# Two transformer blocks on one core: row projections that finish a token half at a time, banks and orders at the seams laid out anew, and two of three products joined into one of 512 columns

## The reference

```python
def first_block(x, mem, ...):
    h = rmsnorm(x, norm_mix)
    fq, fk, fv, ff, gq, gk, gv, gb, ga, gz, sq, sk, sv, gates = split(h @ w_in)
    ya = fox_attention(rmsnorm(fq), rmsnorm(fk), fv, log_sigmoid(ff + bias))   # 4 heads of 128
    yb = rmsnorm(gated_delta_rule(silu(conv(gq, gk, gv)), ...)) * silu(gz)
    yc = stick_breaking_attention(sq, sk, sv)
    g = sigmoid(gates + gate_bias)                                             # 3 x 1024
    x = x + (g[0] * (ya @ w_oa) + g[1] * (yb @ w_ob) + g[2] * (yc @ w_oc)) @ w_out
    x = x + memory_cross_attention(rmsnorm(x), rmsnorm(mem), ...)              # w_mq, w_mkv, w_mo
    return x + conv_ffn(rmsnorm(x), w_up, ffn_conv, w_down)                    # d_ff 2816

def second_block(x, mem, ...):
    x = x + 0.5 * rmsnorm(swiglu(rmsnorm(x), ffn1_w_gate, ffn1_w_up, ffn1_w_down))
    q, k, v, p = split(rmsnorm(x) @ w_in_2)                                    # 512 each
    y = concat(moba_attention(q, k, v), multiscale_pool(p)) @ w_out_2          # 8 heads of 64
    x = x + rmsnorm(y)
    x = x + rmsnorm(memory_cross_attention_2(rmsnorm(x), rmsnorm(mem), ...))   # 4 heads of 256
    return x + 0.5 * rmsnorm(swiglu(rmsnorm(x), ffn2_w_gate, ffn2_w_up, ffn2_w_down))
```

## Time and profile before

| what | value |
|---|---|
| median of three runs | 1312.2 us |
| profiled execution, its own time | 1314.68 us |
| its span on the core | 1313.0 us |
| mean granted TensorE clock | 0.961 of full speed |
| PE busy | 1220.3 us in 8179 matmuls |
| DVE busy | 721.6 us in 797 instructions |
| ACT busy | 631.4 us in 785 instructions |
| HBM read | 191.82 MB, 147 GB/s over the span |

### The profile page before, as it was taken

The page is one execution under the profiler, slowest core; times in us unless marked ns, Lnnn a source line. Parts: engine busy times, 40 slices in busy tenths (PEclk is TensorE's granted clock), DMA queues, the critical chain, the costliest instruction groups (busy, mean ns, idle before and its releaser), DMA issues. The chain is left out here.

```text
span 1313.0 us, 19388 instructions
## 1 busy us (share of the span) xinstructions
PE 1220.3 (93%) x8179; PEld 1116.4 (85%) x8179; DVE 721.6 (55%) x797; ACT 631.4 (48%) x785; POOL 52.5 (4%) x81
## 2 busy tenths in 40 slices
PE   6979999999889989999999999998879987999997
PEld 6967979899888779999889999887857865999985
DVE  6755443643577546788545554445574634555443
ACT  6554434543646746555535444435443634544441
POOL 6001100200000000000000000001000000000000
PEclk9988998999999999999999999998988998999998
DMA  8632222332446434555664555555313424455550
GB/s 241 188 107 97 84 78 73 94 124 97 151 156 209 139 104 157 185 174 189 208 194 157 180 186 172 205 192 167 129 65 114 160 64 144 139 183 193 193 192 32
DMA packets 144142, 194.12 MB, mean 148 GB/s; under 512 B 6136, under 2 KB 121208, under 8 KB 144056
## 3 DMA queue, kind: packets, MB, share of 16 engines
q1 hardware_dynamic: 142856, 188.43, 44.1%
q0 software_dynamic: 1200, 4.46, 1.0%
HBM read 191.82 MB, written 1.05 MB: 147 GB/s over the span
## 5 line engine op out<-in xcount | busy, mean ns | idle before, releaser
L1469 DVE TENSOR_TENSOR wlo<-raw,whi 128x2048 fp32r<-128x2048 f32 x178 | 408.4, 2296 | 293.8 <-ACT whi L1207 293.5
L922 PE MATMUL banks<-xh,whi 128*128 128x256 f32 x1704 | 497.4, 292 | 5.6 <-DVE xl L1486 4.3
L922 PE MATMUL banks<-xl,whi 128*128 128x256 f32 x1704 | 487.3, 286 | 0.0
L922 PE MATMUL banks<-xh,wlo 128*128 128x256 f32 x1704 | 486.9, 286 | 0.0
L1207 ACT ACTIVATE whi<-raw 128x2048 fp32r<-128x2048 f32 x178 | 339.4, 1909 | 203.5 <-PE banks L948 121.1
L922 PEld LDWEIGHTS banks<-xh,whi 128*128 128x128 f32 x1704 | 332.8, 195 | 13.6 <-DVE xl L1486 5.5
L922 PEld LDWEIGHTS banks<-xl,whi 128*128 128x128 f32 x1704 | 332.7, 195 | 1.9 <-issue 1.7
L922 PEld LDWEIGHTS banks<-xh,wlo 128*128 128x128 f32 x1704 | 332.2, 195 | 0.0
L948 PE MATMUL banks<-whi,hh 128*128 128x512 f32 x264 | 102.7, 389 | 0.0
L948 PE MATMUL banks<-wlo,hh 128*128 128x512 f32 x264 | 102.7, 389 | 0.0
L948 PE MATMUL banks<-whi,hl 128*128 128x512 f32 x264 | 102.7, 389 | 0.0
(11 more groups left out here) (362 smaller groups left out, 1538.0 us busy)
## 6 DMA issues: line engine op xcount, KB each, us to landing
raw<-in_w_in SPq DMA_DIRECT2D x40, 1024.0 KB, 5.3
raw<-in_w_up SPq DMA_DIRECT2D x22, 1024.0 KB, 5.1
raw<-in_ffn_w_gate SPq DMA_DIRECT2D x22, 1024.0 KB, 5.4
raw<-in_ffn_w_up SPq DMA_DIRECT2D x22, 1024.0 KB, 5.3
raw<-in_ffn_w_down SPq DMA_DIRECT2D x22, 1024.0 KB, 4.9
raw<-in_w_down SPq DMA_DIRECT2D x11, 1024.0 KB, 4.8
raw<-in_w_out SPq DMA_DIRECT2D x8, 1024.0 KB, 4.9
raw<-in_xa_wkv SPq DMA_DIRECT2D x8, 1024.0 KB, 5.2
```

What stands on the lines that cost most here:

```text
L922: ins = pe.matmul(o, a[:, k, cols_], v[:, k, :], start=(k == 0 and i == 0), stop=(k == KD - 1 and i == 2))
L1469: dve.tensor_tensor(wlo[c % RING][:, :], raw[c % RING][:, :], whi[c % RING][:, :], ALU.subtract).then_inc(dve_done, 1)
```

## The change

**Joined products.** A new kind W takes the place of A in 84 chunks: `fq`, `fk`, `sq`, `sk` and `gz` of the first block, its 12 gate chunks, `mk`, `mq`, the cross attention's keys and queries of the second block, both of its FFNs' gate and up chunks, and the `qk` and `pin` columns of `w_in_2`. `xh` and `xl` lie side by side in `xhl`, so `whi` is multiplied by both in one matmul of 512 columns (L1004 in the changed kernel), and `wlo` by `xh` in one of 256 (L1006): 32 matmuls where there were 48. The result lies in two banks in place of one, and the two halves of a bank, 256 columns each, must be added: `add`, `ga` and `ua`, each a `tensor_reduce` on DVE (L1817, L1824, L1829) that reads 1024 floats of a partition and writes 512. It takes the place of the `copy` on ACT and of the FFN steps' direct reads. The first block's FFN and the convolution stay as they were.

**Half by half.** The last R chunk of a projection does all its products for t = 0 in `mm(c, 0)` and those for t = 1 in `mm(c, 1)`. Residual, `post` steps and norm steps follow for one half at a time, the first beside `mm(c, 1)`.

**Banks.** Each row projection has banks 0 to 3 or 4 to 7, and the transposes of the norm behind it work in the others.

**Orders.** The lanes of the memory attention and of the last cross attention lane are run between the chunks of `w_mo` and `xa_wo_2`, each chunk of which waits for its own heads alone. `w_in_2` starts with the pool's columns; the window sums are a side chain; `w_out_2` takes its rows in the order 2, 3, 0, 1, so that the pool's rows come first. At the FFN seams `nl` goes ahead of the last `add` and of `lo(c + 2)` (`fill_and_turn`).

The diff, cut to its core:

```diff
+    def two_banks():
+
+        turn[0] += 1
+        return (0, 1) if turn[0] % 2 else (2, 3)
...
+    def wide(name, c0, x, evac, banks=None, **k):
+
+        out.append(dict(kind="W", srcs=[((0, 256), kpn(w[name][:, c0:c0 + 256]))], x=x, banks=banks or two_banks(), evac=evac, **k))
...
-    def rows(name, n, x, evac):
-        for j in range(n):
-            out.append(dict(kind="R", j=j, last=j == n - 1, srcs=[((0, 1024), kpn(w[name][256 * j:256 * j + 256, :]))],
-                            x=x, banks=(4, 5, 6, 7), evac=evac if j == n - 1 else None, name=name))
+                            x=x, banks=banks, evac=evac if half else None, **k))
+
+    def rows(name, n, x, evac, base, order=None):
+        for nth, j in enumerate(order or range(n)):
+            out.append(dict(kind="R", j=j, first=nth == 0, last=nth == n - 1,
+                            srcs=[((0, 1024), kpn(w[name][256 * j:256 * j + 256, :]))],
+                            x=x, banks=tuple(range(base, base + 4)), evac=evac if nth == n - 1 else None, name=name))
...
-    ffn(0, "w_up", "w_up", "w_down", DFF)
-    xa_k(3)
-    ffn(1, "ffn1_w_gate_2", "ffn1_w_up_2", "ffn1_w_down_2", 0)
-    xa_v(0)
+            left = KF // 2 - 1 - i
+            if f == 0:
+                b = 2 * (left % 4)
+                cols(gate, 256 * i, "x", (b,), None, f=f, i=i, part="gate")
+                cols(up, c_up + 256 * i, "x", (b + 1,), "ffn", f=f, i=i, part="up")
+            else:
+                b = 4 * ((left + f - 1) % 2)
+                wide(gate, 256 * i, "x", "gate", (b, b + 1), f=f, i=i, part="gate")
+                wide(up, c_up + 256 * i, "x", "ffn", (b + 2, b + 3), f=f, i=i, part="up")
+        rows(down, KF // 2, "h%d" % f, evac, base)
+
+    ffn(0, "w_up", "w_up", "w_down", DFF, "resid", 4)
+    xa_k(3, (2, 3))
+    ffn(1, "ffn1_w_gate_2", "ffn1_w_up_2", "ffn1_w_down_2", 0, "post", 4)
+    xa_v(0, (2, 3))
     win = "w_in_2"
-
+    turn[0] = 0
+    for i in range(2):
+        wide(win, 1536 + 256 * i, "x", "add", to="pin", i=i)
+    for i in (0, 2):
+        wide(win, 256 * i, "x", "add", to="qk", i=i)
     vals(win, 1024, "x", "vcopy", to="bv")
-    for n, i in enumerate((0, 2, 1, 3)):
-        cols(win, 256 * i, "x", (n % 2,), "copy", to="qk", i=i)
-    for i in range(2):
-        cols(win, 1536 + 256 * i, "x", (i % 2,), "copy", to="pin", i=i)
-    rows("w_out_2", 4, "y5", "post")
-    xa_v(1)
+    for i in (1, 3):
+        wide(win, 256 * i, "x", "add", to="qk", i=i)
+    rows("w_out_2", 4, "y5", "post", 0, (2, 3, 0, 1))
+    xa_v(1, (4, 5))
     for i in range(4):
-        cols("xa_wq_2", 256 * i, "x", (i % 2,), "copy", to="xq", i=i)
-    rows("xa_wo_2", 4, "y5", "post")
-    ffn(2, "ffn2_w_gate_2", "ffn2_w_up_2", "ffn2_w_down_2", 0)
+        wide("xa_wq_2", 256 * i, "x", "add", ((6, 7), (0, 1), (2, 3), (0, 1))[i], to="xq", i=i)
+    rows("xa_wo_2", 4, "y5", "post", 0)
+    ffn(2, "ffn2_w_gate_2", "ffn2_w_up_2", "ffn2_w_down_2", 0, "post", 0)
...
+        if ev == "resid":
+            pl.add("dve", "resid", c, 0)
+            pl.add("act", "ns", norm_after(c), 0)
+        elif ev == "post":
+            post(c, 0)
+        for s in mid:
+            place(s)
...
         elif ev == "resid":
-            for t in range(NT):
-                pl.add("dve", "resid", c, t)
+            pl.add("dve", "resid", c, 1)
+            pl.add("act", "nr", norm_after(c), 0)
+            pl.add("act", "ns", norm_after(c), 1)
+            pl.add("dve", "nd", norm_after(c), 0)
+            pl.add("act", "nr", norm_after(c), 1)
+            pl.add("dve", "nd", norm_after(c), 1)
         elif ev == "post":
-            for t in range(NT):
-                pl.add("act", "post1", c, t)
-                pl.add("dve", "post0", c, 1 - t)
-            pl.add("act", "post_r", c)
-            for t in range(NT):
-                pl.add("dve", "post2", c, t)
+            post(c, 1)
...
+    def post(c, t):
+
+        pl.add("act", "post1", c, t)
+        pl.add("dve", "post0", c, t)
+        pl.add("act", "post_r", c, t)
+        pl.add("dve", "post2", c, t)
+        if t and norm_after(c):
+            norm_scale(norm_after(c))
+
+    def norm_scale(name, *ts):
+        for t in ts or range(NT):
             pl.add("act", "ns", name, t)
-        pl.add("act", "nr", name)
-        for t in range(NT):
+            pl.add("act", "nr", name, t)
             pl.add("dve", "nd", name, t)
 
-    def norm_turn(name, into="x"):
+    def fill_and_turn(c, name, base):
+
+        pl.add("act", "hi", c + LEAD)
+        mm(c, early=False, keep=True)
+        norm_turn(name, base)
+        pl.add("dve", "add", c)
+        pl.add("dve", "lo", c + LEAD)
+
+    def norm_turn(name, base, into="x"):
+        pl.norm_base[name] = base
...
-        side.append(sum((attend("moba", h) for h in range(lane, 8, 2)), []))
+        side.append([[]] + sum((attend("moba", h) for h in range(lane, 8, 2)), []))
+    pool_side = [[("dve", "pl_win", g)] for g in range(4)]
+    side.append(pool_side)
     for _ in range(4):
         mm(c)
         c += 1
+    while pool_side:
...
-    ready["y5"] = [("ol", "moba", 6), ("ol", "moba", 7), ("pl_l", 3)]
-    for _ in range(4):
-        mm(c)
-        c += 1
+    for j in range(2):
+        ready["y5", j] = [("ol", "moba", 4 * j + 2), ("ol", "moba", 4 * j + 3)]
+        ready["y5", 2 + j] = [("pl_l", 2 * j + 1)]
+    mm(c)
+    mm(c + 1)
+    drain()
+    mm(c + 2)
+    mm(c + 3)
...
+    for j in range(4):
+        ready["y5", j] = [("ol", "xa", j)]
+    while any(("ol", "xa", 1) == s[1:] for chain in side for link_ in chain for s in link_):
+        hook()
+    mm(c)
+    mm(c + 1)
     drain()
-    ready["y5"] = [("ol", "xa", 2), ("ol", "xa", 3)]
-    for _ in range(4):
-        mm(c)
-        c += 1
+    mm(c + 2)
+    mm(c + 3)
...
-        xh = sb("xh", [P, KD, T], F32R)
-        xl = sb("xl", [P, KD, T], F32R)
+        xhl = sb("xhl", [P, KD, 2, T], F32R)
+        xh, xl = xhl[:, :, 0, :], xhl[:, :, 1, :]
...
+                elif ch["kind"] == "W" and c in plan.fresh and plan.fresh[c]:
+                    both = BOTH[ch["x"]]
+                    for k in range(4 * part, 4 * part + 4):
+                        if k % 2 == 0:
+                            pe.wait_ge(dve_done, at(*plan.fresh[c], k // 2))
+                        for m in range(2):
+                            pe.matmul(bank(b[m]), wh[:, k, m * P:(m + 1) * P], both[:, k, :, :].rearrange("p a t -> p (a t)"),
+                                      start=(k == 0), stop=(k == KD - 1), skip_group_check=True)
+                            ins = pe.matmul(bank(b[m])[:, 0:T], wl[:, k, m * P:(m + 1) * P], Xh[:, k, :], start=False,
+                                            stop=(k == KD - 1), skip_group_check=True)
+                elif ch["kind"] == "W":
+                    o, both = bank(b[part]), BOTH[ch["x"]]
+                    for k in range(KD):
+                        pe.matmul(o, wh[:, k, part * P:(part + 1) * P], both[:, k, :, :].rearrange("p a t -> p (a t)"),
+                                  start=(k == 0), stop=(k == KD - 1), skip_group_check=True)
+                        ins = pe.matmul(o[:, 0:T], wl[:, k, part * P:(part + 1) * P], Xh[:, k, :], start=False, stop=(k == KD - 1),
+                                        skip_group_check=True)
...
+                    for half in range(2):
+                        t, q = (part, half) if ch["last"] else (half, part)
+                        for kk in (0, 1) if ch["last"] else (q,):
+                            k = 2 * ch["j"] + kk
+                            for nb in (q,) if ch["last"] else (0, 1):
+                                for i, (v, a) in enumerate(((Xh, wh), (Xh, wl), (Xl, wh))):
+                                    ins = pe.matmul(bank(b[2 * t + nb]), v[:, k, t * P:(t + 1) * P],
+                                                    a[:, kk, nb * 512:(nb + 1) * 512],
+                                                    start=(ch["first"] and kk == 0 and i == 0),
+                                                    stop=(ch["last"] and kk == 1 and i == 2))
...
+                for step in plan.bank_wait[("pl_mm", g)]:
+                    pe.wait_ge(DONE[plan.engine[step[0]]], at(*step))
+                pe.matmul(pool_bank(g), poolw[:, g, :], pin[:, g, :], start=True, stop=True).then_inc(pe_done, 1)
...
+                act.wait_ge(dve_done, at("add", chunk_of("gate", 11)))
+                for f in range(8):
+                    ins = act.activation(g[:, f, :], g[:, f, :], ACT.Sigmoid, bias=pcolumn("gate_bias", 8 * br + f))
...
+                act.wait_ge(pe_done, at("mm", c, t))
+                act.wait_ge(pe_done, at("nt", LAST_NORM[c], 3))
+                act.activation(xs[:, t, :], row_banks(c, t), ACT.Square, accum_out=ms[:, t:t + 1]).then_inc(act_done, 1)
+
+            def post_r(c, t):
+                link(act.activation(rn[:, t:t + 1], ms[:, t:t + 1], ACT.Ln, bias=eps, scale=1.0 / D))
```

(25 more changed lines are left out.)

259 lines of the change are left out of this document (111 added, 148 removed).

## The result

The changed kernel takes 1277.0 us, the median of four executions (1273.8 to 1284.9), where the kernel before took 1314.0 (1312.1 to 1320.0): a ratio of 0.972, interval 0.969 to 0.976. A second set of four gave 0.972 as well (0.969 to 0.976). The gain is 37 us; the forecast was 50. The range of 1246 to 1283 holds the time, the band that was given 0.58, 1254 to 1272, does not. The profiled execution is the longest of the first four, 1284.9 us with a span of 1283.2.

A forecast was written before the change was run, and what follows sets the result against it. PE was taken as the bound: matmul rate in full stretches plus its waits at seams and lanes. Terms summed to -49.7 us, from a median of 1312.2 to 1262 (band 1254 to 1272, chance 0.58); range 1246 to 1283.

The forecast's parts named there:

- (a): Rival on W chunks: the joined pair is no faster than the three matmuls; 1281 us, or 1278; chance 0.08.
- (c): Rival on DVE: the reduce costs 2.4 us, FFNs hold but some 13 places wait for an add; 1278 us; chance 0.07.
- (d): Rival: slow reduces across two banks make DVE the bound; 1325 us at three times 1.224; chance 0.03.
- 16 x (226.8 + 120.5): W chunk's matmul time in ns, each size at its uniform-stream rate: 5.56 us against 5.79, -19.2 us over 84 chunks.
- gain beside square: Step in the walk of the seam behind xa_wo_2: gain runs beside the square, 1.25 us; that seam's term was -2.9.
- its largest term: Last cross attention lane run between matmuls of xa_wo_2: fewer waits and less half clock, -9.2 us.
- The 3.9 us for the windows: Moba stage loss: the first two groups' window sums stand ahead of the first lanes' sm on DVE, +3.9 us.
- (b): Rival: DVE's queue eats the moba stage's gain, so its 7.0 us goes; 1269 us; chance 0.11.
- norm_xq -0.9: Seam at norm_xq, between w_out and the first FFN: the half-by-half start gains 0.9 us.
- mem_g_2 -0.5: Seam at mem_g_2, between w_out and the first FFN: the half-by-half start gains 0.5 us.
- (e): Rival: fewer waits keep the clock up longer, restoring twice what was booked, 12 us more; 1250 us; chance 0.08.
- (f): Rival: halves' chains and lanes wait as before, only joined products count; 1293 us; chance 0.05, of which 0.02 with (a).

The follow-up runs named there:

- twice: Changed kernel with each reduce of the second block's two FFNs run twice over the same banks; 1279.1 us.
- split: Changed kernel with each joined 512-column matmul split into two of 256; its sums are wrong, only time is read; 1290.5 us, 0.981 of before.
- whole: Changed kernel with the half-by-half order of last row chunks and their residual, post and norm steps undone; 1289.1 us, 0.980 of before.
- drained: Changed kernel with the last memory and cross attention lanes run out before w_mo and xa_wo_2 again; 1288.2 us, 0.982 of before.
- poolbanks: Changed kernel with four banks for the pool's four products instead of two in turn; 1277.4 us, 0.973 of before.
- poolmid: Changed kernel with window sums behind the lanes' pn and the pool's products moved up in two pairs; 1275.5 us, 0.969 of before.
- poolbehind: Changed kernel with the window sums behind the lanes' pn on DVE instead of ahead of sm; 1278.4 us, 0.974 of before.
- memfix: Changed kernel with norm_mem's turn ahead of the half's residual and banks 2 and 3 for mv; 1276.5 us, 0.973 of before.

## Why the prediction was right, and where it was off

The forecast was -49.7 us and the profiled execution gave -29.8, the medians -37. That 1277 lies in the range is in part luck: the range reached up to 1283 for the sake of rivals (a) and (c), neither of which came, and what filled it were terms that fell short for other reasons. By stages, in the profiled executions:

| stretch | forecast | measured |
|---|---|---|
| first block's projections, to the O chunks | -5.8 | -3.3 |
| O chunks | -0.8 | -1.5 |
| `w_out` to the first FFN | -8.2 | +2.3 |
| seam behind the first FFN | -0.9 | -1.4 |
| gate and up, second block's first FFN | -5.0 | -2.4 |
| to the end of `w_out_2` | -8.4 | -5.4 |
| cross attention | -10.7 | -10.7 |
| seam behind it | -2.9 | -2.6 |
| gate and up, last FFN | -5.0 | -2.8 |
| the end | -1.9 | -2.0 |

The forecast column is the prediction's terms, with 0.229 us for each W chunk of the stretch, laid to the stretch they belong to; the end of `xa_wo_2` is taken at the end of its last matmul in both kernels. Two rows are the clock's as much as the change's. The first block took 313.1 to 321.6 us in the ten traces that leave it as the changed kernel has it, so its -3.3 says little. And the O chunks took 40.1 us in eight of the later traces, as in before, and 38.6 only where the clock stayed up.

**The reduce** was right, 1224 to 1225 ns for 1.22 us, and it hides under PE, with nearly all of a second one (`twice`). Rivals (c) and (d) are out. The rule of the Trainium skill (VectorE: DVE Perf Modes, "Rules for kernel authors") that `tensor_reduce` is the slowest DVE operation made no difference here: an elementwise step of 1024 took as long.

**Joined products**: the mechanism was right and the size depends. `split` shows that the join carries it. The term that was mis-sized is 16 x (226.8 + 120.5) a chunk: a pair of 347.3 ns was forecast, 346.7 is what one of two levels shows, 353.3 the other, and the profiled execution had the slow one in both FFNs. There the 22 chunks save 2.4 us and not 5.0; in seven of the eight later traces with the alternating order the last FFN's save 4.5 to 5.8 against before's 127.9, some of it clock in their first chunk. Rival (a) is out at either level. So is the formula of the Trainium skill (TensorE: Matmul & The Clock Gate, "Back-to-back issue gap", where it stands for a single matmul by itself), by which a stretch would have gained 352 x 2.6 ns = 0.9 us, an estimate: even the slow level gains 2.4.

**Seams and end** were right to 0.3 us in sum, by `whole` for the right reason. One step in the walk was wrong: "gain beside square". In the changed kernel `post0` waits for `post1` of its half, and that for a reason: both read the same two banks, where the kernel before could set one half's gain beside the other half's square. The Trainium skill says of this (PSUM — Partial Sum Buffer, "PSUM bank collisions raise a hardware error") that no two engines may access one bank in the same partitions at once; no run here tried it. The first transpose came 6.8 us behind the end of the last matmul where 6.5 were forecast, and the seam took 10.1 us from there where 9.8 were.

**Cross attention** was right, and so was its largest term. From the last scores to the end of `xa_wo_2` the trace has 26.4 us (1054.56 to 1081.00), where before had 35.6 and 26 were forecast: 9.1 us for the 9.2. `drained` splits them. There the same piece takes 31.8 us (1054.74 to 1086.52), so 5.3 are the matmuls between the steps of the lane. The other 3.8 fit what `drained` keeps and before has not, that each chunk waits for its own heads alone: in `drained` the first product of `xa_wo_2` starts at 1063.65, while the last values are still multiplied, where before waited 1.90 us for `y5l` and then ran 3.4 us at half clock. At the start of the stage, the seam behind `w_out_2` gained 1.0 us (15.2 to 14.2 up to the first query chunk) where 1.75 was booked.

**Moba stage**: -8.4 were forecast and -5.4 came, at the upper end of what this stage takes (122.7 to 126.8 in the seven other traces that leave the pool as it is). The prediction said that the pool's wait of 2.68 us goes. It grew to 4.9: the products take turns in two banks, the third waits until `pl_l` of the first has read its bank, and that stands on DVE behind `sm` and `pn` of the next lanes. No step of the prediction asked what stands ahead of `pl_l`. `poolbanks` moves the wait and `poolmid` removes it. Of the last lanes' wait of 4.96 us, 4.0 was to go, and 2.35 stayed. The 3.9 us for the windows were not measured: `poolbehind` put them elsewhere, and the sum of the lanes' waits did not change. Rival (b) thus came in part, by its route (DVE's order) but at other places than the first `sm`.

**`w_out` to the first FFN** is the step that failed: -8.2 were forecast and +2.3 came. Two terms in it were right. The memory lanes took 17.4 us from the last scores to the end of `w_mo` where before had 21.1, 3.7 for the 3.9 forecast (18.8 in `drained`, so 1.4 of it is interleaving), and the last chunk with norm_ffn gained 1.5, as forecast with its joined chunk. What failed are norm_xq -0.9 and mem_g_2 -0.5, each walked against a free ACT, a free DVE and free banks. From the first matmul of `w_out` to the first of `mk` the trace has 28.1 us in place of 25.3, and from the product of `mv` to the first key chunk 9.6 in place of 5.0. Three things stand behind this:

- The residual and squares of half 0 stand ahead of `nh` of norm_mem (2.6 us of wait).
- The copy of `mv` is in banks 0 and 1, which the first transposes of mem_g_2 need; before had it in 2 and 3, so that half of them ran ahead of it (3.7 us of wait, where before had 1.7).
- The first key chunk lies in banks 2 and 3, where the last two groups of these transposes lie, so it waits until `nl` has read all four groups (2.3 us). Before's chunk lay in bank 0 and waited for the first group alone. In `memfix` the same chunk falls into banks 0 and 1, and the wait is 1.1.

The clock fell at the longer two of these waits, for 3.4 and 10.2 us; 17 us of this stretch were at the lower level, before 10. `memfix` took one of the waits away and shortened two, and got others. What would have to move for this stretch to gain stays open.

**The clock**: rival (e), twice what was booked, did not come: the mean went from 0.961 to 0.967 in the profiled executions. But the executions differ by the clock. The first block ran in 321.6 us and in 313.1 (`poolbanks`, where nothing of it is altered); see below. Rival (f) is out by `whole` and `drained`.

## What to carry to other kernels

When steps are split into halves so that one half's chain starts early, list on each engine what now stands behind it: a seam's gain is real only where nothing else was due there, and two norms in flight push each other. A bank used in turns is a queue; when its reader moves to a busy engine's list, the next product waits for everything that stands ahead of that reader. A product that takes two banks waits for the later of their two readers: look where they fall behind a norm's transposes. And price a mixture of two matmul sizes by its own measured start-to-start time, not by the sum of two uniform streams, or keep both levels in the range.

## What the runs showed of the hardware

**A stream of alternating 512- and 256-column matmuls has two steady levels.** 353.3 or 346.7 ns a pair, kept for a whole stretch of 352 pairs at full clock. Two executions of one program had the last stretch at different levels (125.1 and 122.8 us), and the two stretches of one execution can differ. Of the nine traces with the alternating order and single reduces, the first stretch has the slow level in eight and the last stretch the fast one in seven. What chooses it was not tried. Streams of one size (120.5 and 226.8) showed one level each.

**The same work runs with the clock low for more or less of its time.** The first block's projections at both ends, nothing in them altered (windows: poolbanks; the changed kernel's is above):

```profile
14.81:327.91 313.10, 295.14 (x1800) 252.70 (x1801) 196.54 (x249) 140.57 (x189) 34.13 (x30) 0.98 0.37 116
```
Mean granted clock 0.98 in 313.1 us, 0.95 in 321.6. The time at the lower level there was 13.7 us in the one and 34.1 in the other, in pieces of 3.4 and 6.8 us. The same waits of PE stand in both, and the fall does not need one. Of the eight pieces in the longer trace two come at a wait (6.7 and 2.0 us) and one 8 us behind a wait of 0.7; ahead of the other five PE has no wait over 0.1 us for 10 us and more. The first of the five (windows, changed kernel):

```profile
143.65:147.07 3.42, 3.42 (x15) 1.97 (x14) 1.96 (x1) 0.00 (x0) 0.00 (x0) 1.00 0.11 12
147.07:150.48 3.41, 3.41 (x14) 3.12 (x15) 1.38 (x2) 1.46 (x4) 1.28 (x1) 0.50 0.87 295
```
Ahead of it PE ran the twelve matmuls of two score steps, eight of them on 4 partitions, without a gap; why the clock falls there in one trace and not in another is not shown. The eight executions of the changed kernel bear it out: the longest, 1284.9 us, had a mean clock of 0.967, the shortest, 1273.8, had 0.975. An estimate from these, with PE busy all the while, is 10.6 us between them, nearly all of their difference of 11. It is the reason why a change of 4 us is read from stages here and not from one time, and why even a stage needs more than one trace.
